# In tile 0, the low halves of weight tiles 18 to 33 are made by VectorE instead of GpSimd

## What is computed

```python
h = rmsnorm(x, w_norm_pre[l])
proj = h @ w_in[l]                                   # 2048 x 1024 by 1024 x 3328
q_a, k_a, v_a, z_a, q_r, f_r, i_r, z_r = jnp.split(proj, SPLIT_POINTS, axis=-1)
o_a = sliding_window_sink_attention(rope(q_a), rope(k_a), v_a, sinks) * jax.nn.silu(z_a)
o_r = hgrn2_chunkwise(q_r, f_r, i_r, lb)             # 4 heads of 128, chunks of 64
o_r = rmsnorm(o_r, hgrn_norm[l]) * jax.nn.silu(z_r)
y = jnp.concatenate([o_a, o_r], axis=-1) @ w_out[l]
x = x + rmsnorm(y, w_norm_post[l])
```

## Time and profile before

| | us |
|---|---|
| median of 3 runs | 949.74 (949.72 to 950.84) |
| the profiled execution, its time | 949.19 |
| the profiled execution, its span | 947.4 |
| PE busy (matmuls) | 912.0 (96%) |
| DVE busy | 551.1 (58%) |
| ACT busy | 376.6 (40%) |
| POOL busy | 273.6 (29%) |

### The profile page before, as it was taken

How to read it: one execution, slowest core, us unless ns; L and a number is a source line. 1 busy time by engine, 2 the same in 40 slices (tenths; PEclk the granted TensorE clock), 3 DMA queues, 4 the chain that set the end, 5 groups by cost and what they waited for, 6 DMA issues and landing times.

```text
span 947.4 us, 12091 instructions
## 1 busy us (share of the span) xinstructions
PE 912.0 (96%) x4496; PEld 745.1 (79%) x4496; DVE 551.1 (58%) x954; ACT 376.6 (40%) x736; POOL 273.6 (29%) x174
## 2 busy tenths in 40 slices
PE   7798999979999999999999999999999999999996
PEld 4686778768878878888888878788888887888885
DVE  7676786667265668465432676566424566844523
ACT  6126455736340434445320253445412053444322
POOL 3345535755370111253020011334102011213102
PEclk9998999999999999999999999999999999999998
DMA  7388655553988843344479744344378743334344
GB/s 272 111 313 293 200 182 172 202 183 109 402 324 276 301 175 134 134 158 176 178 252 332 254 172 154 111 159 174 115 270 330 254 159 127 115 134 178 139 175 176
DMA packets 56331, 191.26 MB, mean 202 GB/s; under 512 B 7120, under 2 KB 7376, under 8 KB 56272
## 3 DMA queue, kind: packets, MB, share of 16 engines
q1 hardware_dynamic: 48832, 176.18, 51.4%
q10 hardware_dynamic: 7440, 14.30, 4.3%
HBM read 141.18 MB, written 44.04 MB: 196 GB/s over the span
## 4 chain that ended last, share of the span: by engine, by line
PE 74%; DVE 10%; DMA 4%; POOL 4%; issue 3%; ACT 3%; ACTq 1%; SPq 0%; DVEq 0%; POOLq 0%
PE bank L408 43%; PE bank L417 18%; PE bank L432 3%; DMA kept_lo<-w_lo 2%; PE bank L448 2%; POOL w_lo L1056 2%; PE bank L442 1%; PE bank L469 1%; PE bank L481 1%; PE bank L483 1%; PE bank L473 1%; DVE q_gate L1044 1%; DVE x_acc L816 1%; DMA f_d<-f_c 1%; DVE read_state L897 1%
## 5 line engine op out<-in xcount | busy, mean ns | idle before, releaser
L408 PE MATMUL bank<-h_hi,w_hi 128*128 128x512 f32 x832 | 333.9, 401 | 3.7 <-DVE h_lo L782 3.4
L408 PE MATMUL bank<-h_hi,w_lo 128*128 128x512 f32 x832 | 330.3, 397 | 0.0
L408 PE MATMUL bank<-h_lo,w_hi 128*128 128x512 f32 x832 | 327.0, 393 | 0.0
L408 PEld LDWEIGHTS bank<-h_hi,w_hi 128*128 128x128 f32 x832 | 157.3, 189 | 50.7 <-issue 16.1
L408 PEld LDWEIGHTS bank<-h_lo,w_hi 128*128 128x128 f32 x832 | 157.4, 189 | 31.8
L408 PEld LDWEIGHTS bank<-h_hi,w_lo 128*128 128x128 f32 x832 | 157.7, 189 | 30.5 <-issue 1.2
L1056 POOL TENSOR_TENSOR w_lo<-w_raw,w_hi 128x1024 fp32r<-128x1024 f32 x39 | 95.5, 2454 | 117.4 <-ACT w_hi L591 117.4
L1061 POOL TENSOR_TENSOR probs<-probs,s_stats 128x512 f32<-128x512 f32 x32 | 37.1, 1160 | 293.6 <-DVE s_stats L935 293.6
L417 PE MATMUL bank<-w_lo,mix_hi 128*128 128x512 f32 x256 | 100.0, 391 | 0.0
L417 PE MATMUL bank<-w_hi,mix_lo 128*128 128x512 f32 x256 | 100.0, 391 | 0.0
L417 PE MATMUL bank<-w_hi,mix_hi 128*128 128x512 f32 x256 | 99.7, 389 | 0.0
(11 more groups left out here) (148 smaller groups left out, 1300.3 us busy)
## 6 DMA issues: line engine op xcount, KB each, us to landing
w_hi<-kept_hi SPq DMA_DIRECT2D x96, 512.0 KB, 3.6
w_lo<-kept_lo SPq DMA_DIRECT2D x96, 512.0 KB, 4.5
w_raw<-in_weights SPq DMA_DIRECT2D x40, 512.0 KB, 4.3
kept_hi<-w_hi SPq DMA_DIRECT2D x34, 512.0 KB, 5.4
kept_lo<-w_lo SPq DMA_DIRECT2D x34, 512.0 KB, 6.1
x_in<-in_x SPq DMA_DIRECT2D x16, 512.0 KB, 7.0
x_in<-in_x_rows SPq DMA_DIRECT2D x8, 1024.0 KB, 7.3
out<-q_gate ACTq DMA_DIRECT2D x12, 512.0 KB, 7.6
```

The lines of the kernel that those rows point to most:

```text
L408: mm = pe.matmul(acc(w)[:, :], stationary[:, s, k, :], moving[:, k, :], start=(m == 0), stop=(m == 3 * KT - 1), skip_group_check=True)
```

## The change

The low halves of weight tiles 18 to 33 of tile 0 (`DVE_LOW`) are made by DVE, at the end of its step, with the same instruction and the same wait for `hi_split`. POOL makes 1 to 17, and 34 to 39 in tile 1, as before. Where the maker changes (tiles 18 and 34) the new one also waits for the counter `lo_split`, so that the counts keep their order. `splits` now gives the number `i` instead of `w`, which changes nothing in what ACT does.

```diff
 def splits(t, s):
 
-    return [w for w in split_at(s) if t * WT + w < FRESH]
+    return [t * WT + w for w in split_at(s) if t * WT + w < FRESH]
...
+DVE_LOW = range(H0 + 8, WT)
...
+            def split_lo(i):
+                dve.wait_ge(hi_split.sem, hi_split.after(0, 0) + i)
+                if i in (DVE_LOW.start, DVE_LOW.stop):
+
+                    dve.wait_ge(lo_split.sem, lo_split.after(0, 0) + i - 1)
+                s = SPLIT_SLOT[i % WT]
+                dve.tensor_tensor(w_lo[:, s, :, :], w_raw[:, i % RAW_SLOTS, :, :], w_hi[:, s, :, :], ALU.subtract).then_inc(lo_split.sem, 1)
...
+                    for i in splits(t, s):
+                        if i in DVE_LOW:
+                            split_lo(i)
+
                     if s == OUT0 + 4:
                         for b in range(4):
                             copy_y(t, 0, b)
...
             def split_lo(i):
                 pool.wait_ge(hi_split.sem, hi_split.after(0, 0) + i)
+                if i in (DVE_LOW.start, DVE_LOW.stop):
+
+                    pool.wait_ge(lo_split.sem, lo_split.after(0, 0) + i - 1)
...
-                    for w in splits(t, s):
-                        split_lo(t * WT + w)
+                    for i in splits(t, s):
+                        if i not in DVE_LOW:
+                            split_lo(i)
```

More of the change, by code:

```diff
@@ L672, in _ @@
                     if s == K_TILE + 1:
-                        for w in splits(t, s):
-                            split_hi(t * WT + w)
+                        for i in splits(t, s):
+                            split_hi(i)
                     if s - 1 in ROPE_TILES:
@@ L715, in _ @@
                             act.activation(mix_hi[:, QT + head, :], h_mix[:, :], ACT.Copy).then_inc(mixh_hi.sem, 1)
-                    for w in splits(t, s) if s != K_TILE + 1 else ():
-                        split_hi(t * WT + w)
+                    for i in splits(t, s) if s != K_TILE + 1 else ():
+                        split_hi(i)
                     if 3 <= c < CHUNKS:
```

## The result

Six runs of the change have a median of **941.02 us** (940.22 to 941.42), six of the kernel before on the same chip 949.73 (948.31 to 950.84). The ratio is 0.990, 95% interval 0.989 to 0.991: 8.7 us faster. The prediction was 939.6 with a range of 937.4 to 943.6. The profiled execution took 940.84 us, with a span of 939.0.

A forecast was written before the change was run, and what follows sets the result against it. PE, busy 912.0 of 947.4 us, was taken as the bound. Window gains 1.0 + 2.3 + 5.6 + 1.2 = 10.1 off the profiled 949.19 gave 939.1, plus 0.55 for the median: 939.6 us, range 937.4 to 943.6.

The forecast's parts named there:

- The bound and the yardstick: PE's idle time bounds the gain; tiles 1 to 3 are the yardstick, tile 0's four windows losing 12.3 us.
- Windows one and two: Tile 0's first two windows: stalls before L448, L490 and L457 go, gains of 1.0 and 2.3 us.
- (a): Third window, slack 0.84 us behind L1091: a new stall of 0.3 us before L490, 0.5 with its restart.
- (b): Third window, slack 1.42 us behind v_r: a new stall of 0 to 0.9 us before L462, taken as 0.5.
- rival A: POOL's operations hold DVE's moved splits: 1.29 us more at two places, no gain at L401; 943.2 us, chance 16%.
- Term 6: Fourth window, PE's 1.0 us stall before L401: gain 1.2 of 1.53 us, bounds 0 and 1.5.
- Costed at nothing: SP's queue, where raw loads and saves wait for the same low halves: priced at no time.
- rival B: DVE inherits the waits for ACT's w_hi: costs 12.4 us against the gain of 10.1; 952.0 us, chance 4%.
- C: Rival: the same matmuls then wait for ACT, so the time stays near 949.5 us; chance 3%.
- The split's price: Each of the 16 low halves added to DVE takes 1.16 us, 18.6 us in all.
- Rival D: All the loss goes but 0.7 us before the first moved tile: gain 11.6, 938.1 us; chance 12%.
- term 3: First window: the 0.8 us stall before L448 goes, gain 1.0 us; the rest of its 1.93 stays.

The follow-up runs named there:

- fb_first: The change, with DVE's split of a gate step (tiles 21 and 25) made right behind the next step's f_b instead of in front of it: 938.14 us.
- x_later: The change, with POOL's x_acc in the last head of tile 0 waiting until DVE has written v_r: 939.76 us.
- end_pool: The change, with the low halves of tiles 31 to 33 given back to POOL: 941.78 us.
- last_free_wide: fb_first with DVE also making tiles 12 to 17 and, in the last head alone, the query step's split moved behind v_r: 937.14 us.
- pool_reads: The change, with POOL running a useless SBUF-reading multiplication in place of each low half 18 to 30: 958.43 us.

## Why the prediction was right, and where it was off

**The bound and the yardstick** held. Tile 1's windows as the floor gave 26.71 and 26.73 for what came out as 27.28 and 26.74, and the measured gain, 8.7 us, lies 1.4 under the 10.1 forecast.

**Windows one and two**: 1.0 and 2.3 forecast, 0.91 and 2.27 measured.

**(a)** 0.5 with restart forecast, 0.57 measured: a gap of 0.28 us in a window of 27.28 us, where tile 1's has 26.71. fb_first shows that the split before f_b makes it.

**(b) is the term that was mis-sized.** "A stall between 0 and 0.9 before L462. I take the middle, 0.5": it is 1.46 us, 1.71 with the restart (62.41 - 60.70), outside the bounds given. They were built from the splits' own time alone and asked only whether k_mid or f_d gets the lock. What lay on top of tile 1 were 0.96 us by k_mid on f_d and 0.62 by x_acc on L923 (1.78 against the 1.16 that it has there); x_later takes the second away altogether, 1.10 us. With 1.7 in place of 0.5 the sum would have been 8.9 us, and the windows gave 9.01. That the measured time still lies in the range is owed to the range's width, and not to this term. What came is rival A's mechanism at one of its two places, at 1.6 over tile 1 where it was priced at 1.29. Its other parts, the same hold at (a) and no gain before L401, did not come.

**Term 6** gave its upper bound, 1.53 without (b), not 1.2, and one of its two reasons has fallen for the last three tiles. The w_hi that waited 2.64 us for a save in the earlier trace rows waits as long now:

```profile
250.25 1.06 ACT L593 ACTIVATE w_hi<-w_raw 128x1024 fp32r<-128x1024 f32 x1 [2.69 <-DMA kept_lo<-w_lo]
...
266.29 1.02 PE L403 MATMUL bank<-x_acc,ones_r 128*128 128x512 f32 x2
```

and end_pool keeps the gain with POOL making the last three. Counted from the start of the window and less the 1.71 us that PE lost in it, this w_hi starts at 44.7 us, against 46.7 before: the chain of splits is 2 us sooner there. Whether that is the residual's load behind the shorter read_state, as the other reason said, no run isolates. In last_free_wide, where PE loses nothing before, L403 also starts without a wait, 60.70 us after the window's start: the gain is no side effect of a late PE.

**Costed at nothing**: SP's queue and the waits for w_hi. In tile 0 that was right. DVE does stand 8.8 us at its splits for w_hi, 8.1 of them in three waits behind 230 us, but no wait of PE stands behind these; rival B did not come, nor C. PE's wait for reloaded weights early in tile 1 (L410, 0.2 us before) is absent with the change and up to 1.0 in variants.

**The split's price** was taken as 1.16 us from the one row that there was. The group of the change's instructions that write w_lo:

```profile
L1073 POOL TENSOR_TENSOR w_lo<-w_raw,w_hi x23: 2375/2399/2911, 10.6 to 270.6; 128x1024 fp32r<-128x1024 f32 x23
L794 DVE TENSOR_TENSOR w_lo<-w_raw,w_hi x16: 1211/1222/2067, 138.3 to 243.9; 128x1024 fp32r<-128x1024 f32 x16
```

The median is 1.222 us. The Trainium skill (VectorE: DVE Perf Modes, "The TRN2 errata") gives (N+151)/0.96 ns for an fp32 tensor_tensor, by which 1.22 us is the estimate for N=1024. It was nearer than the row. Two of the sixteen took about 2 us, beside POOL operations that had gone in first.

**Rival D's 0.7 us** for the steps before the first moved tile does not fit term 3, which leaves 0.93 of the first window's 1.93. By that D's time would be 938.3 instead of 938.1. The first window kept 1.02 of its loss in the change and none in the three variants that also move tiles 12 to 17.

**Outside the windows** nothing was forecast, and the two profiles differ there by 1.09 us at the start and -1.7 at the end. The gaps before tile 0's first matmuls differ between all profiles, whatever was changed, and so does the granted clock there: from 80 to 100 us it is 0.83 before and 0.91 in the change. The 2.1 us before L444 follow a wait of DVE for a DMA of tile 3's rope (`f_a L862 <- DMA f_b<-f_a`, 4.35 us); the kernel before has waits of that kind there too, and no gap, so the cause is not shown; a gap before L444 behind 300 us, of 0.3 to 2.1 us, was there in six of the eleven experiments' profiles, in four of them in tile 3, and absent in the other five and in the one of before. Whether the change makes it likelier can't be said from one profile each, and it stays open.

## What to carry to other kernels

Where GpSimd and VectorE both read SBUF, price an instruction by whom it shuts out, and not only by its place in its own queue: thirteen useless instructions on POOL cost 3.0 us of tile 0's first three windows when they only wrote and 11.7 us when they read. When work moves to the engine that is waited for, put it where that engine waits for another anyway (behind f_b and not before it, 1.2 us in the windows). In estimating a new stall, lay the other engine's short operations over the new timeline, each as a possible hold of 1 us, before bounding it by the moved work alone. And compare variants by windows between the same matmuls: the medians put fb_first 2.9 us under the change where the edit was worth 1.2.

## What the runs showed of the hardware

- A scan of 1.23 us stays 1.23 beside POOL's memsets and becomes 2.26 beside its multiply. The Trainium skill (SBUF — State Buffer, "Who interferes with whom") says that a GpSimd instruction that only writes does not contend with a DVE one of two SBUF inputs, and the trace agrees.
- The hold doesn't shrink with the held instruction: a copy of 128x4 takes 1.07 us under L1108, in tile 1 as in tile 0. The shortest of its sixteen takes 0.17.
- The exclusion works in both directions within one window: a DVE split of 2.28 us beside two mix_lo of 3.52 us together.
- A stall of PE costs 0.24 to 0.3 us more than its gap, with the granted clock at 1.00. Over the lengths without a gap, 26.71 and 60.70 (last_free_wide), a gap of 0.28 costs 0.57 and one of 1.46 costs 1.71 (the change), 0.36 costs 0.60 (x_later), and 0.80 costs 1.05 (fb_first).
- After a stall of 3.7 us in pool_reads the granted clock averaged 0.70 and 0.73 over the next two stretches of 3 us, and was 1.00 again behind them.
- The multiply of 128x1024 on POOL takes 1.89 us and the subtraction that writes the fp32r type 2.40; a memset of that size takes 0.95.
